# Hybrid attention and retention layer on one core: how the first norm's weight reaches the chip, and the order of ScalarE's first evacuations

## What is computed

```
def rmsnorm(x, g):
    y = xf * lax.rsqrt(jnp.mean(xf * xf, axis=-1, keepdims=True) + EPS)
    return (y * g.astype(jnp.float32)).astype(x.dtype)
...
        h = rmsnorm(x, norm_mix_pre[l])
        proj = jnp.einsum('bsd,dn->bsn', h, w_in[l])
```

## Time and profile before

| what | value |
|---|---|
| time, median of 3 runs | 630.76 us (630.18 to 631.71) |
| time of the profiled execution | 631.34 us |
| its span | 629.5 us |
| TensorE busy | 619.4 us (98% of the span) |
| VectorE busy | 420.6 us (67%) |
| ScalarE busy | 314.0 us (50%) |
| GpSimd busy | 98.1 us (16%) |

### The profile page before, as it was taken

The page is one execution under the profiler, slowest core; times in us unless marked ns, Lnnn a source line. Parts: engine busy times, 40 slices in busy tenths (PEclk is TensorE's granted clock), DMA queues, the critical chain, the costliest instruction groups (busy, mean ns, idle before and its releaser), DMA issues.

```text
span 629.5 us, 8647 instructions
## 1 busy us (share of the span) xinstructions
PE 619.4 (98%) x3062; PEld 511.7 (81%) x3062; DVE 420.6 (67%) x621; ACT 314.0 (50%) x505; POOL 98.1 (16%) x110
## 2 busy tenths in 40 slices
PE   8999999999999999999999999999999999999996
PEld 7887878778787877899888888888888888888885
DVE  3657449647865876884755556566565668988786
ACT  5557338526735834664533334343333336656661
POOL 4313103112210402420000000000000013532203
PEclk9999999999999999999999999999999999999999
DMA  9834223331512354642433233333323436999923
GB/s 274 239 102 134 67 68 101 100 100 50 150 33 100 121 197 151 199 136 68 133 94 104 74 97 98 100 100 97 103 86 101 166 67 111 188 223 228 232 87 133
DMA packets 91947, 78.90 MB, mean 125 GB/s; under 512 B 2617, under 2 KB 76521, under 8 KB 91922
## 3 DMA queue, kind: packets, MB, share of 16 engines
q1 hardware_dynamic: 84434, 61.79, 32.2%
q0 software_dynamic: 7488, 16.80, 13.2%
HBM read 76.46 MB, written 2.12 MB: 125 GB/s over the span
## 4 chain that ended last, share of the span: by engine, by line
PE 91%; DVE 3%; POOL 2%; DMA 1%; issue 1%; ACT 1%; DVEq 0%; SPq 0%; POOLq 0%; ACTq 0%
PE bank L537 82%; PE bank L679 1%; PE bank L617 1%; DMA gains<-in_norm_mix_pre_dram 1%; PE bank L548 1%; POOL grstd L471 1%; PE bank L668 1%; DVE xs L1326 1%; PE bank L608 1%; PE bank L607 1%; POOL work L475 1%; PE bank L658 1%; PE bank L657 1%; DVE yT L1255 1%; DVE gvar L1295 0%
## 5 line engine op out<-in xcount | busy, mean ns | idle before, releaser
L537 PE MATMUL bank<-hT,ws 128*128 128x512 f32 (+1 forms) x1872 | 410.3, 375 | 0.7 <-DVE work L1304 0.6
L537 PEld LDWEIGHTS bank<-hT,ws 128*128 128x128 f32 x1872 | 328.8, 188 | 61.7 <-issue 2.5
L1208 DVE TENSOR_TENSOR ws<-raw,ws 128x1024 fp32r<-128x1024 f32 x87 | 106.2, 1222 | 7.1 <-ACT ws L894 6.7
L537 PE MATMUL bank<-ws,yT 128*128 128x512 f32 x468 | 109.9, 391 | 0.0
L537 PEld LDWEIGHTS bank<-ws,yT 128*128 128x128 f32 x468 | 87.0, 188 | 18.2 <-issue 0.4
L894 ACT ACTIVATE ws<-raw 128x1024 fp32r<-128x1024 f32 x88 | 92.6, 1054 | 15.6 <-PE bank L537 11.5
L1115 ACT ACTIVATE gains<-bank,conv 128x512 f32<-128x512 f32 x22 | 17.2, 781 | 76.8 <-PE bank L537 76.8
L1470 DVE SCALAR_TENSOR_TENSOR gains<-bank,conv,gains 128x511 f32<-128x511 f32 x22 | 16.5, 750 | 53.8 <-ACT gains L1115 53.8
L520 POOL DMA_DIRECT2D late<-in_w_down_dram x8 | 10.7, 1335 | 253.2 <-DVE ws L1510 253.2
L1115 ACT ACTIVATE rot<-bank,conv 128x512 f32<-128x512 f32 x22 | 17.2, 780 | 63.7 <-PE bank L537 63.7
L537 PE MATMUL bank<-ws,hT 128*128 128x512 f32 x186 | 42.8, 389 | 0.0
(11 more groups left out here) (135 smaller groups left out, 597.4 us busy)
## 6 DMA issues: line engine op xcount, KB each, us to landing
raw<-in_w_up_dram SPq DMA_DIRECT2D x44, 512.0 KB, 3.8
raw<-in_w_in_dram SPq DMA_DIRECT2D x28, 512.0 KB, 4.4
raw<-in_w_out_dram SPq DMA_DIRECT2D x16, 512.0 KB, 3.5
raw<-in_w_down_dram POOLq DMA_DIRECT2D x12, 512.0 KB, 7.7
raw<-in_w_down_dram SPq DMA_DIRECT2D x9, 512.0 KB, 4.0
late<-in_w_down_dram POOLq DMA_DIRECT2D x8, 512.0 KB, 5.9
xs<-in_x_dram SPq DMA_DIRECT2D x6, 512.0 KB, 4.1
late<-in_w_down_dram SPq DMA_DIRECT2D x6, 512.0 KB, 6.9
```

What stands on the lines that cost most here:

```text
L537: return nc.tensor.matmul(dst, st, mv, start=start, stop=stop, skip_group_check=onto)
L1208: nc.vector.tensor_tensor(ws[:, c, 1, :], raw[:, c, :], f32(ws[:, c, 0, :]), ALU.subtract).then_inc(w_lo, 1)
```

## The change

Three things change.

1. The norm's weight now comes as one row of 1024 values on one partition (4 KB, `gain_row`), issued by SyncE ahead of everything else. VectorE sets a row of 128 ones. TensorE multiplies the ones by the two halves of the row, which puts the row on all 128 partitions in PSUM banks 6 and 7. VectorE copies both banks to `gains`, and `normed_rows(0)` waits for these copies.
2. TensorE's filler ahead of `turn_rows(0)` was `warm(22)`. It is now `warm(6)`, the two products, and `warm(24)`.
3. On ScalarE `h_evacuate(0)` now stands ahead of `split_hi(0)`.

```
@@ buffers
+        gain_row, ones = work[0:1, 8192:8192 + D], work[0:1, 9216:9216 + P]
@@ SyncE
+            sp.dma_start(gain_row, norm_mix_pre).then_inc(gains_loaded, 16)
             load_x(0)
             load_x(1)
-            sp.dma_start(gains[:, 0, :], norm_mix_pre[0].partition_broadcast(P)).then_inc(gains_loaded, 16)
             load_turn(0, 0, 1)
@@ TensorE
             pe.wait_ge(ident_set, 2)
-            warm(22)
+            warm(6)
+            pe.wait_ge(ones_set, 1)
+            pe.wait_ge(gains_loaded, 16)
+            for half in range(2):
+                nc.tensor.matmul(bank[6 + half][:], ones, gain_row[:, 512 * half:512 * half + 512],
+                                 start=True, stop=True).then_inc(gains_spread, 1)
+            warm(24)
             turn_rows(0)
             warm(2)
             turn_rows(1)
@@ ScalarE
             x_in(0)
             x_in(1)
+            h_evacuate(0)
             split_hi(0)
-            h_evacuate(0)
             h_evacuate(1)
@@ VectorE
-            dve.wait_ge(gains_loaded, 16)
+            nc.vector.memset(ones, 1.0).then_inc(ones_set, 1)
+            for half in range(2):
+                dve.wait_ge(gains_spread, half + 1)
+                nc.vector.tensor_copy(gains[:, 0, 512 * half:512 * half + 512], bank[6 + half][:]).then_inc(gains_ready, 1)
+            dve.wait_ge(gains_ready, 2)
             normed_rows(0)
             normed_rows(1)
```

More of the change, by code:

```diff
@@ L278, in build @@
         ident_set = sem("ident_set")
+        ones_set, gains_spread, gains_ready = sem("ones_set"), sem("gains_spread"), sem("gains_ready")
         conv_turned, conv_ready = sem("conv_turned"), sem("conv_ready")
```

## The result

The changed kernel takes 637.83 us, median of 9 runs (634.18 to 638.74), against 631.00 for the kernel before, median of 9 (630.18 to 631.71): a ratio of 1.0092, 95% interval 1.0069 to 1.0116. It is slower, as forecast, but by 6.8 us in place of 2.7, and the median lies outside the predicted range. The nine times are in two groups with nothing between: 634.18, 634.35, 634.47, and six from 637.80 to 638.74. The profile that came with the result is of the upper group (638.74 us, span 636.9).

What follows compares the result with a forecast made beforehand. TensorE was taken to bound the kernel, its first turning setting the time. A later first turning (+2.2 us) and ScalarE's order (+0.5) sum to +2.7 on 630.76, giving 633.5 us; 8-in-10 range 631.8 to 635.4.

Steps and rivals of the forecast that it cites:

- The first turning is what counts: TensorE's first turning of rows, at 9.92 us before: a microsecond won or lost there goes nearly whole into the time.
- The slack that the prediction named as a way to be wrong: Sign of error: first turning at 12.1 us but the span's end moved by under 1.5 us, slack the waits don't show.
- 12 passes to 4.77, the row landed in time: TensorE's opening: 12 filler passes end at 4.77 us and cover the row's DMA, needed at 4.56, by 0.4 us.
- The four wide passes end at 6.75: The two products on TensorE: 1.1 passes until the clock rises at 5.5 us, 2.9 fast ones after, ending at 6.75.
- The floor and the ceiling: First turning: 10.3 us, 0.4 later, with all passes at 2.4 GHz; 13.3, +3.4, with the four wide passes at 1.2 GHz.
- rises later: Rival: TensorE's clock rises later because the products use one row; wide passes all slow give 634.7 us; chance 0.15.
- Its extreme, all 48 passes slow: Extreme of the later rise: all 48 filler passes behind the products slow too (10.2 us), about 639.6 us.
- The rule on the slow start: TensorE's opening: slow products vary from run to run; the changed kernel pays half of each microsecond the rise comes later.
- VectorE 0.9 us earlier and unused: VectorE's copies end at 7.6 us and `normed_rows(0)` starts there, not at 8.58; 0.9 us won, unused behind TensorE's filler.
- ScalarE's order, +0.6 us at the third turning: Evacuating tile 0 first delays GpSimd's low part and tile 2's rows, so the third turning waits 0.6 us; 0.5 taken.
- The median: Whole kernel: median of 630.76 + 2.7 = 633.5 us, 0.4% slower.

Runs made afterwards that it cites:

- e3: The kernel before with 38 filler products in place of 22, nothing else: 633.97 us median, ratio 1.0043.
- e7: The changed kernel with the weight's row on partition 96 and zeros above it, so the two products use 97 rows: 634.77 us median, ratio 1.0056.
- e1: The changed kernel with the two wide products taken from the identity and ones on 128 rows, norm's weight left out: 634.21, 634.47, 635.04 and 636.34 us.
- e5: The kernel before with its 22 filler products replaced by 22 products of one row of ones by one row of ones: 635.56 us median, ratio 1.0067.
- e8: The changed kernel with the weight's row on partition 96 (97 rows), 9 filler products in place of 24, and ScalarE's old order: 632.82 us median, ratio 1.0021.
- e10: The changed kernel with 97 rows and 9 filler products in place of 24, keeping its new ScalarE order: 631.58 us median, ratio 1.0013.
- e2: The changed kernel with 18 filler products ahead of the two products and 12 behind, in place of 6 and 24: 634.68, 635.03, 637.01, 637.27 us.

## Why the prediction was right or wrong

- **The first turning is what counts.** Right: 6.77 us there, 7.4 in the span. A longer list alone (e3) passed through whole. The slack that the prediction named as a way to be wrong isn't there. That the change is slower was no luck: a list longer by about as much gives it without any product on one row.
- **12 passes to 4.77, the row landed in time.** Right: the row's DMA is never waited for; the products start at 4.70 to 4.71, 0.14 us behind the slot. The loading of their weights starts only at 4.70 too, while on 97 rows it ran under the last filler pass, from 4.36, and the products kept the slot (4.57, e7).
- **The four wide passes end at 6.75.** This is the step that failed. It took the rise of the clock at 5.5 us from the trace and placed it in a list with other work in it. The working is right for 128 rows (e1: 6.87, first turning 12.23 for 12.13) and for the lower group (6.61, and 12.07; its fourth turning is 2.74 us later than before, the forecast). 11 of 17 executions are in the upper group. In the three of them with a trace the rise isn't there: the wide passes end at 8.4, and the filler behind them runs slowly for 4.5 to 6 us more, which puts the turning at 16.0 to 16.7.
- **The floor and the ceiling.** The ceiling of +3.4 us held only the wide passes at the low clock and let the filler be fast behind them. The measured term is +6.1 to +6.8. The rival "rises later" named the cause, products on one row, with a chance of 0.15, but was priced as if the rise came the moment the products were over. Its extreme, all 48 passes slow, was left out of the range; the measured turnings are 55 to 70% of the way from the ceiling to it. The chance had no row behind it: the opening of before holds no pass on one row, and an unseen kind of work on the engine that bounds the kernel deserved a wider upper end.
- **The rule on the slow start.** The Trainium skill, "TensorE: Matmul & The Clock Gate", Part 1 (The HAM clock gate), says that the slow stretch is a matter of time and not of the number of products. For passes on 128 or 97 rows the runs don't speak against it: rises at 5.35 to 7.90 us, scattered, with passes of 128 columns alone and with four of 512 among them. For passes on one row they do: 9.7 us of them without a pause brought none (e5). The measurement decides.
- **VectorE 0.9 us earlier and unused.** Right for the lower group (copies end at 7.4, rows start at 7.44). In the upper one the rows start at 9.25, later than the 8.58 of before, so the change doesn't even bring what it puts in place of the broadcast.
- **ScalarE's order, +0.6 us at the third turning.** Right in mechanism and size: the distance from the first to the third turning grows from 6.92 to 7.43 us, to the fourth from 9.70 to 10.30. (One reading was off: TensorE gets to the first term at 13.88, T + 4.0 and not T + 4.2. No wait came of it.) What was missed is its other side: it keeps GpSimd's low part away from VectorE's rows (e8 against e10). With the first turning near 12 or 16 us there is nothing to protect: VectorE's rows are ready over 3 us ahead of their turnings (9.9 and 11.7), and the meeting in e8 costs 2.1.
- **The median.** 631.0 + 3.3 is the lower group, against 2.7 forecast; its trace has 2.74 at the fourth turning and 3.0 in the span, and where the rest comes from is open. The upper group adds 3.5 to 4.4 more.

Open is what decides between the groups in one execution, why the lower one's rise comes earlier than any other, and the upper values of e1 and e2. That e10 stays 0.6 us above the kernel before by the medians while the two profiles agree to 0.2 us has a likely reason: the profiled execution is e10's fastest, with an early rise (5.9 us). In e8, with the same list up to there, the rise is at 7.4 and the first turning at 9.96 in place of 9.20. The kernel before had 1.17 us of waiting to absorb that; this one hasn't. No trace of e10 near its median is there to show it.

## What to carry to other kernels

Filler that warms TensorE and work that has to be done early are not the same thing: a product with a contraction of one row kept TensorE busy here and left it at 1.2 GHz. Pad it with zeros (97 of 128 rows were enough; nothing between 1 and 97 was tried), or put it where the clock is already up. Ahead of the first real work count every pass that is added, at the low clock too, since on a kernel that TensorE bounds each one is paid in full (e3). When an engine's early work comes free sooner, look at which other engine it now meets.

## What the runs showed that was not expected

- Passes on one row of the array: 44 of them in 9.75 us, no rise, and then 4.7 us more of passes on 128 rows before it came. With passes on 97 rows among those on 128 the rise came as with 128 throughout.
- The recorded granted clock is full scale in stretches in which the passes are 0.213 us apart. The clock's records in the trace begin only at the rise, and what the page prints ahead of them is no measurement: at the start the spacing tells the level.
- The rise varies from run to run: 5.35 to 7.90 us in the eleven traces that open with passes on 97 or 128 rows, 3.5 to 6.1 us behind the first pass. The kernel before covers this by its wait for the broadcast; variants with a short list can't, and their times spread more (630.6 to 634.3 in e8). How much of that spread is the rise isn't measured.
- GpSimd's subtraction and VectorE's row operation, both with two operands in SBUF, held each other up: 3.29 us for 2.37, and 4.58 for 2.48 as a pair. The times fit one waiting for the other to end, not sharing: VectorE's first operation took 1.28 us as ever, GpSimd lost 0.92, and VectorE's second ended at 13.20, 1.08 us behind GpSimd's end at 12.12. The Trainium skill, "SBUF — State Buffer", section "SBUF: two separate sides", says the same: the pair of ports which the two engines share is locked for a whole instruction.
